# A four-stage streaming encoder: three FFN chunks instead of four before the block products, and one weight sum by a copy and an adding DMA

## What is computed

```python
def swiglu(x, g, w_gu, w_down):
    gu = rmsnorm(x, g) @ w_gu                              # 1024 -> 2 x 2816
    return (jax.nn.silu(gu[..., :D_FF]) * gu[..., D_FF:]) @ w_down   # 2816 -> 1024

        x = x + jnp.concatenate([op, om], axis=-1) @ w_out[i]
        x = x + swiglu(x, g_ffn[i], w_gu[i], w_down[i])
```

## Time and profile before

| | us |
|---|---|
| median of 3 runs | 1207.27 |
| lowest, highest | 1207.05, 1207.91 |
| the profiled execution, own time | 1208.02 |
| its span in the trace | 1206.3 |
| TensorE busy in the span | 1197.1 |
| VectorE busy | 979.7 |
| ScalarE busy | 641.6 |

### The profile page before, as it was taken

One profiled execution on the slowest core, in us unless ns is written; L12 is line 12 of the kernel. 1 busy time (PEld: TensorE's weight loads), 2 busy tenths in 40 slices (PEclk: granted clock), 3 DMA queues, 4 the chain that ended last, 5 costly groups with the idle time before them and its releaser, 6 DMA issues.

```text
span 1206.3 us, 22717 instructions
## 1 busy us (share of the span) xinstructions
PE 1197.1 (99%) x8853; PEld 1152.8 (96%) x8853; DVE 979.7 (81%) x1585; ACT 641.6 (53%) x1136; POOL 78.5 (7%) x111
## 2 busy tenths in 40 slices
PE   8999999999999999999999999999999999999998
PEld 8998999999999999999987887899999999999998
DVE  5777458999999999976674777557999999999973
ACT  6657335455555555545672567434555555455543
POOL 2000000002001000102001100000001000100200
PEclk9999999999999999999999999999999999999999
DMA  7343222236334433526434110333134433532533
GB/s 249 108 140 105 71 78 83 74 89 136 106 88 113 121 97 91 133 80 173 137 107 140 57 41 2 105 88 88 53 101 115 120 97 94 130 105 80 131 85 105
DMA packets 195242, 124.08 MB, mean 103 GB/s; under 512 B 6339, under 2 KB 185891, under 8 KB 194880
## 3 DMA queue, kind: packets, MB, share of 16 engines
q1 hardware_dynamic: 183904, 103.30, 28.9%
q0 software_dynamic: 11040, 19.27, 7.4%
q10 hardware_dynamic: 192, 0.06, 0.0%
HBM read 106.70 MB, written 7.94 MB: 95 GB/s over the span
## 4 chain that ended last, share of the span: by engine, by line
PE 93%; DVE 3%; ACT 1%; DMA 1%; issue 1%; SPq 0%; DVEq 0%; ACTq 0%
PE ACCP L2016 28%; PE ACCP L2037 24%; PE MISC L2037 23%; PE ACCP L2173 3%; PE ACCP L2196 3%; PE ACCP L2366 2%; PE ACCP L2341 2%; PE MISC L2055 1%; PE MISC L2302 1%; PE MISC L2315 1%; DMA XR<-in_x_prompt 1%; PE MISC L2061 1%; PE ACCP L2078 1%; PE ACCP L2092 1%; DMA PC<-PC 0%
## 5 line engine op out<-in xcount | busy, mean ns | idle before, releaser
L1179 ACT ACTIVATE WH<-RAW 128x1024 fp32r<-128x1024 f32 (+2 forms) x149 | 144.2, 968 | 145.8 <-PE ACCP L2016 93.5
L1197 ACT ACTIVATE EH<-SB 128x1024 fp32r<-128x1024 f32 (+1 forms) x116 | 112.5, 970 | 163.2 <-DVE SB L1568 82.8
L1543 DVE TENSOR_TENSOR WL<-RAW,WH 128x1024 fp32r<-128x1024 f32 (+2 forms) x148 | 165.8, 1120 | 30.8 <-ACT WH L1179 29.7
L1574 DVE TENSOR_TENSOR EL<-SB,EH 128x1024 fp32r<-128x1024 f32 (+1 forms) x116 | 128.7, 1109 | 5.5 <-ACT EH L1197 3.7
L2037 PE MATMUL MISC<-BH,EH 128*128 128x288 f32 x360 | 106.7, 296 | 0.0
L2037 PE MATMUL ACCP<-BH,EH 128*128 128x288 f32 x360 | 106.6, 296 | 0.0
L2037 PE MATMUL MISC<-BL,EH 128*128 128x288 f32 x360 | 106.2, 295 | 0.0
L2037 PE MATMUL ACCP<-BL,EH 128*128 128x288 f32 x360 | 106.2, 295 | 0.0
L2037 PE MATMUL ACCP<-BH,EL 128*128 128x288 f32 x360 | 105.8, 294 | 0.0
L2037 PE MATMUL MISC<-BH,EL 128*128 128x288 f32 x360 | 105.8, 294 | 0.0
L2016 PE MATMUL ACCP<-XH,WH 128*128 128x288 f32 x480 | 104.1, 298 | 0.0
(11 more groups left out here) (411 smaller groups left out, 3432.0 us busy)
## 6 DMA issues: line engine op xcount, KB each, us to landing
RAW<-in_w_gu SPq DMA_DIRECT2D x88, 512.0 KB, 4.1
RAW<-in_w_down SPq DMA_DIRECT2D x48, 384.0 KB, 4.1
RAW<-in_w_in SPq DMA_DIRECT2D x16, 512.0 KB, 4.2
RAW<-in_w_mem_kv SPq DMA_DIRECT2D x16, 512.0 KB, 3.8
RAW<-in_w_out SPq DMA_DIRECT2D x16, 512.0 KB, 3.8
X<-PC POOLq DMA_DIRECT2D x48, 144.0 KB, 3.2
RAW<-in_w_down SPq DMA_DIRECT2D x16, 256.0 KB, 3.0
RAW<-in_w_kv SPq DMA_DIRECT2D x8, 512.0 KB, 3.6
```

The lines of the kernel that those rows point to most:

```text
L1179: a.activation(panel_in(WH, w % SPLIT_SLOTS, p), panel_in(RAW, p % RAW_SLOTS, p), ACT.Copy).then_inc(split_ready(w, True)[0], 1)
L1197: a.activation(EH[:, first:first + n, 0:nh], mixtures(s)[:, first:first + n, 0:nh], ACT.Copy).then_inc(block_hi, n)
L1543: v.tensor_tensor(panel_in(WL, w % SPLIT_SLOTS, p), panel_in(RAW, p % RAW_SLOTS, p), panel_in(WH, w % SPLIT_SLOTS, p), ALU.subtract).then_ ...
L1574: v.tensor_tensor(EL[:, first:first + n, 0:nh], mixtures(s)[:, first:first + n, 0:nh], EH[:, first:first + n, 0:nh], ALU.subtract).then_in ...
```

## The change

In each layer `LEADS` goes from 4 to 3 and what hangs on it is put in another order:

- Chunk 3 is multiplied as a pair. Pair 0 is now chunk 3, pairs 1 to 3 are chunks 4 to 6, and the first down pair is pair 4.
- Pair 0's mixtures are made ahead of the first plain panel's other work (`prepare_pair`, `prepare_fourth`), and its panels are loaded early (`load_first`), so that two of the four `RAW` slots are taken until pair 0, and the panels of plain chunks 1 and 2 take turns in the other two (`slot_of`).
- The last of the seven activation blocks gets its low part inside pair 0 (`token_lo`).
- The mixing of hidden chunks 0 and 1 (`mix_blocks`, `blocks_hi`, `blocks_lo`) moves from the time of the plain panels into that of pair 1, that of chunks 2 and 3 into pair 2, that of 4 and 5 into pair 3.
- For pairs 1, 2 and 3 (`BY_DMA = 3`) VectorE's `mix_1` is dropped. ScalarE copies the first half of the second panel into `SB` (`copy_for_sum`), and POOL starts a software DMA that adds the second half to it. `mix_2` and ScalarE's `EH` copies wait for that DMA (`first_mixed`). In the time of the pair before, `blocks_lo` goes ahead of `mix_2`.

```diff
-    LEADS = 4
+    LEADS = 3
+    BY_DMA = 3
@@ feed_forward: prepare, one row of the table
-                   (2, 1): [("lo", 4), ("lo", 5), ("pair", count["pair"]), ("blocks_hi", k0)],
+                   (2, 1): [("lo", 5)]}
...
                     steps.append(r_step)
+                    add("prepare_pair", k=count["pair"], s=r_step.s)
                     add("prepare_scale", layer=layer, k=0)
                     add("prepare_scale", layer=layer, k=1)
+                    add("prepare_fourth", k=count["pair"])
...
-            if n == 1:
-                k = k0 + LEADS // 2 - 1
+            if n in (1, 2):
+                k = k0 + n - 1
...
+        def mixtures_made(s, n):
+            own = sum(3 if steps_of_pair[i].z is not None else 4 for i in range(s.i))
+            if s.z is None:
+                return [(mixed, own + n)]
+            return [(first_mixed, 16 * (s.z + 1))] + ([(mixed, own + n - 1)] if n > 1 else [])
@@ gpsimd, pair
+                    after = steps_of_pair[s.i + 1]
+                    if after.z is not None:
+                        k1, k2, nh = inputs_of(after)
+                        gp.wait_ge(*raw_there(after.p + 1))
+                        gp.wait_ge(mix_copied, after.z + 1)
+                        gp.dma_start(SB[:, 0, 0:nh], raw_panel(after.p + 1)[:, k2], accum_op=ALU.add).then_inc(first_mixed, 16)
                     gp.wait_ge(copied, 3 * s.i + 3)
                     gp.dma_start(PC[:, s.i % 2, 2], PC[:, s.i % 2, 1], accum_op=ALU.add).then_inc(kept_summed, 16)
@@ scalar
+            def copy_for_sum(s, prev):
+                k1, k2, nh = inputs_of(s)
+                act.wait_ge(*raw_there(s.p + 1))
+                act.wait_ge(block_lo, 5 * prev.i + 2)
+                a.activation(SB[:, 0, 0:nh], raw_panel(s.p + 1)[:, k1], ACT.Copy).then_inc(mix_copied, 1)
...
                     mix_hi_22(s)
+                    if s.nxt and steps_of_pair[s.i + 1].z is not None:
+                        copy_for_sum(steps_of_pair[s.i + 1], s)
@@ vector, pair
                     if s.alone:
                         dve.wait_ge(panel_used, s.before.q + 1)
-                        for n in range(4):
+                        for n in range(3):
                             mix_lo(s, n, 1)
+                        token_lo(s.layer, NB - 1)
+                        mix_lo(s, 3, 1)
...
+                    by_dma = after and after.z is not None
                     if after:
-                        mix_1(after)
+                        if not by_dma:
+                            mix_1(after)
                         mix_3(after)
                     if not s.alone:
                         mix_lo_22(s)
+                    if by_dma and s.k is not None:
+                        blocks_lo(s.k)
                     if after:
                         mix_2(after)
-                    if s.k is not None:
+                    if not by_dma and s.k is not None:
                         blocks_lo(s.k)
```

More of the change, by code:

```diff
@@ L158, in encoder_kernel @@
              "zero": 0, "win": 0, "r": 0, "h": 0, "pool": 0, "bank": 0, "wide_sq": 0, "wide_norm": 0,
-             "plain": 0, "split": 0, "pair": 0, "gu": 0, "down": 0, "added": 0, "kept": 0}
+             "plain": 0, "split": 0, "pair": 0, "gu": 0, "down": 0, "added": 0, "kept": 0, "summed": 0}
     panel_shape, splits, raw_free = [], [], []
+    slot_of = {}
     units_before, sq_of_norm, job_of_wide, branch_bank = {}, {}, [], {}
@@ L325, in feed_forward @@
                     **panel((up_of if e else gate_of)(j), KC))
+                if (j, e) == (0, 1):
+                    first_pair = take("panel", 2)
+                    panel_shape.extend([(KC, P)] * 2)
+                    raw_free.extend([("pair", count["pair"])] * 2)
+                    add("load_first", p=first_pair, view=gate_of(LEADS), ys=up_of(LEADS))
                 for what, k in prepare[j, e]:
                     add("prepare_" + what, layer=layer, k=k)
+        for n in range(2):
+            slot_of[first_pair + 4 + n] = (first_pair + 2 + n) % RAW_SLOTS
+        last_lead = next(s for s in reversed(steps) if s.kind == "lead")
         order, waiting = [], []
@@ L337, in feed_forward @@
         for n, (which, j, part) in enumerate(order):
-            i, p, w = take("pair"), take("panel", 2), take("split")
+            i, w = take("pair"), take("split")
             nk = KC if which == "gu" else PARTS[part][1] - PARTS[part][0]
-            panel_shape.extend([(nk, P)] * 2)
+            if n:
+                p = take("panel", 2)
+                panel_shape.extend([(nk, P)] * 2)
+                raw_free.extend([("pair", i)] * 2)
+            else:
+                p = first_pair
             splits.append(("pair", p, i))
-            raw_free.extend([("pair", i)] * 2)
             prev = steps_of_pair[i - 1] if n else None
@@ L360, in feed_forward @@
                 h=layer * FC + j if which == "gu" else None, prev=prev, nxt=n + 1 < len(order),
-                alone=n == 0, bank=n % 2, side=count["acc"] % 2, before=steps[-1] if n == 0 else None,
+                alone=n == 0, bank=n % 2, side=count["acc"] % 2, before=last_lead if n == 0 else None,
                 m=count["job"], g=count["acc"], made=made, k=k,
-                first=which == "down" and j == 0)
+                first=which == "down" and j == 0, z=take("summed") if 0 < n <= BY_DMA else None)
             steps_of_pair[i] = steps[-1]
@@ L832, in moving_of @@
             return {"x": (XH, XL, xl_ready, T), "y": (HH, HL, yl_ready, T)}[kind]
+        raw_slot, raw_before, users = [], [], [[] for _ in range(RAW_SLOTS)]
+        for p in range(len(panel_shape)):
+            slot = slot_of.get(p, p % RAW_SLOTS)
+            raw_slot.append(slot)
+            raw_before.append(users[slot][-1] if users[slot] else None)
+            users[slot].append(p)
         def panel_in(slots, slot, p):
@@ L1009, in load @@
             def load(p, src):
-                if p >= RAW_SLOTS:
-                    sp.wait_ge(*raw_released(p - RAW_SLOTS))
-                sp.dma_start(panel_in(RAW, p % RAW_SLOTS, p), src()).then_inc(raw_loaded[p % RAW_SLOTS], 16)
+                if raw_before[p] is not None:
+                    sp.wait_ge(*raw_released(raw_before[p]))
+                sp.dma_start(panel_in(RAW, raw_slot[p], p), src()).then_inc(raw_loaded[raw_slot[p]], 16)
             for tt in X_ORDER:
@@ L1041, in _ @@
                         sp.dma_start(yp[:, 2:TT, D - P:D], YST[1][:, 2:TT]).then_inc(y_last_stored, 16)
-                elif s.kind == "pair":
+                elif s.kind == "load_first" or s.kind == "pair" and not s.alone:
                     load(s.p, s.view)
@@ L1191, in mix_hi @@
             def mix_hi(s, first, n):
-                act.wait_ge(mixed, 4 * s.i + first + n)
+                for made in mixtures_made(s, first + n):
+                    act.wait_ge(*made)
                 if s.i:
@@ L1560, in mix_2 @@
                 k1, k2, nh = inputs_of(s)
-                dve.wait_ge(mixed, 4 * s.i + 1)
+                for made in mixtures_made(s, 1):
+                    dve.wait_ge(*made)
                 v.tensor_tensor(mixtures(s)[:, 2, 0:nh], mixtures(s)[:, 0, 0:nh], raw_panel(s.p)[:, k1], ALU.subtract).then_inc(mixed, 1)
@@ L1566, in mix_4 @@
                 k1, k2, nh = inputs_of(s)
-                dve.wait_ge(mixed, 4 * s.i + 3)
+                for made in mixtures_made(s, 3):
+                    dve.wait_ge(*made)
                 v.tensor_tensor(mixtures(s)[:, 3, 0:nh], raw_panel(s.p)[:, k2], mixtures(s)[:, 2, 0:nh], ALU.subtract).then_inc(mixed, 1)
@@ L1945, in _ @@
                     mix_2(first)
-                    mix_4(first)
+                elif s.kind == "prepare_fourth":
+                    mix_4(steps_of_pair[s.k])
                 elif s.kind == "hl":
```

31 lines of the change are left out of this document (13 added, 18 removed), and 3 rows, old and new, of the table prepare.

## The result

The changed kernel takes 1213.7 us (median of 4 runs, 1213.3 to 1213.97) against 1207.45 of the kernel before beside it (4 runs, 1207.05 to 1207.91). The ratio is 1.0051, with a 95% interval of 1.0039 to 1.0062: slower by half a per cent, and 1213.2 had been predicted, in a range of 1209.0 to 1217.5. The profiled execution took 1213.73 with a span of 1212.0; before it was 1208.02 and 1206.3, so the two profiles differ by 5.71.

The account below looks back on a forecast made before the run. VectorE's pace in pairs 1 to 3 was taken to bound the kernel; 2.28 + 1.99 + 2 x 0.45 + 2 x 0.4 = +5.97 us on the median of 1207.27 made 1213.2, range 1209.0 to 1217.5.

Parts of the forecast that it names:

- What TensorE saves: Per layer 96 plain matmuls (12.79 us) become a pair of 84 (11.20 us): 1.6 us saved if nothing waits.
- The plain stretch: Plain panels before pair 0: VectorE has about 30 us of work in 31.8, so the cost is nothing.
- Pair 0: VectorE crosses pair 0 12.37 us after its start (11.70 before); the new DMA is wanted at 8.45.
- The transfers: Waits for software DMAs around pair 0: 0.4 us a layer, between bounds of nothing and 1.3.
- The bound of 1.3: Upper bound a layer on waiting for the new DMA in pair 0: landing 5.65 + 0.5 against 4.9 allowed.
- The step of 13.55: VectorE's time between crossings in pairs 1 and 2: 12.70 - 0.60 + 0.60 (`WL` wait) + 0.85 (`HBL` wait).
- Pair 3 and the down pair: 9.92 us from the crossing to the first down matmul; a third sum behind it costs 0.45 a layer.
- The sum: All terms over both layers: 2.28 + 1.99 + 2 x 0.45 + 2 x 0.4 = +5.97 us.
- TensorE's saving: Rival: VectorE keeps near TensorE's pace in pairs 1 and 2, with no waits 1202.4 us; chance 0.06.
- The waits on ScalarE: Rival: these two waits in pairs 1 and 2 don't arise, step 12.10, about 1207.4; absent or half as large: 0.09.
- The transfers issued in pairs 1 and 2: Rival: DMAs late in every step, pairs 1 and 2 lose 0.7 each, 3.8 a layer in all, 1220; chance 0.11.
- the rival that the prediction drew from it: VectorE's two-port mode blocks GpSimd's descriptors: each DMA takes 2.5 us more, pair 0 is 0.8 late; no chance given.

Follow-up runs that it names:

- the reordered one: Changed kernel with ScalarE's copy behind `WH`, `HBH` and `HBL` behind the first two `EH` and `EL`, sums alternating, and the down pair's work reordered: 1206.71 us.

## Why the prediction was right

- **What TensorE saves**, 1.6 us a layer: right in what there is to save, 12 matmuls a layer; all of it and more is given back as waits.
- **The plain stretch**, nothing: right. The last `BL` ahead of pair 0 ended at 213.04 (211.69 + 1.35) and TensorE went from the last plain matmuls (212.78) to pair 0 (213.05) without a pause; in layer 1 it is 860.02 and 860.03. VectorE was busy for 30.4 of the 31.75 us from the first row behind R to pair 0, where 30 of 31.8 had been estimated, so the cover was 1.3 us and not some 2.
- **Pair 0**, crossed at +12.37: 12.45 in layer 1. The copy ended at +3.4 (3.5 predicted), but GpSimd issued the transfer only at +4.03 (217.08 - 213.05), and it took 4.0 us where I had 3.2 alone. That was enough, by 0.6: it landed at 221.1, and ScalarE began the `EH` copy, which waited for `mix_3`, at 221.66 (+8.61, where 8.45 had been predicted).
- **The transfers**, 0.4 a layer: the sum of 0.8 came near the net 0.9 by luck. Nobody waited for the new transfers; what was late was the kept sum, in layer 0 alone, by 1.63 of waiting. The prediction had given the kept sum about 6.4 us and charged it nothing of its own; it had 6.1 (the sum that waits would have started at 225.11, 0.55 behind the one at 224.56, and the transfer was issued at 219.01), and it took 7.6. The bound of 1.3 was worked out for the new transfer, from 5.65, the longest landing of the first kept sum that I had looked at the earlier trace rows. The queue behind the new transfer was in the reasoning and is worth some 0.5; the loads beside it do the rest, in layer 0 perhaps with the instruction packet.
- **The step of 13.55**: measured 13.55 in three of the four steps, and 12.93 behind the late sum. The waits cost 0.61 and 0.84 by the distance of starts, where I had 0.6 and 0.85; the rows show them as 0.52 and 0.76, without the 0.08 by which instructions overlap when nothing waits. The two runs with one order changed confirm each term apart, and the run without sums by transfer has the 12.70 that the working began with.
- **Pair 3 and the down pair**, 9.92 from crossing to first matmul: 9.91 in both layers. The third sum and `EL` 3 and 4 behind it: 0.45 predicted, 0.45 and 0.48 measured.
- **The sum**, +5.97: 6.2 by the down pairs' rows, 5.71 between the profiles, 6.25 between the medians.
- **The rivals**: TensorE's saving never showed: the step was 13.55, and even the steps of 12.03, just under the 12.1 at which the layers were to break even, gave a time equal to before. The waits on ScalarE arose. The transfers issued in pairs 1 and 2 were in time in the changed kernel. In the reordered one VectorE waited at most 0.18 for one, but ScalarE's `EH` copy waited 1.72 and 1.91 for the one issued in pair 1, so they are at the edge there.
- **The rules weighed.** The fit of the Trainium skill, "DMA: Bandwidth & Descriptors" (Anatomy of one DMA), gives 2.6 us for 256 KB, an estimate from its figures. The new transfer took 3.2 without loads beside it and 4.0 ahead of them, 0.6 and 1.4 more than the fit, yet nobody waited for it: the charge that stayed was borne out by the kept sum, not by it. The block of GpSimd's descriptors by VectorE, from "SBUF — State Buffer" (SBUF: two separate sides), isn't seen in this kernel: with VectorE busy around them, GpSimd's issue rows last 0.85 to 0.92 us. That page of the Trainium skill ties the block to a two-port mode, and under "Who interferes with whom" it says that `tensor_tensor` has none. VectorE's rows around these issues are all `TENSOR_TENSOR`, so the page's rule gave no block here, and the rival that the prediction drew from it didn't follow; the rows agree with the page.

```profile
217.08 0.92 POOL L1186 DMA_DIRECT2D SB<-RAW  x1 [113.47 <-ACT SB L1242]
219.01 0.86 POOL L1188 DMA_DIRECT2D PC<-PC  x1 [1.00 <-ACT PC L1257]
227.46 0.85 POOL L1186 DMA_DIRECT2D SB<-RAW  x1 [7.59 <-ACT SB L1242]
```
